# A quarter of the down weights multiplied in f32 straight from the raw buffer, and the gate/up biases added by VectorE

## The chip, the core and the metric

The kernel runs on one core of one Trainium2 chip. The metric is the device time of one execution in microseconds (us). Three executions of the kernel before gave a median of 1267.36 us (1266.95 to 1268.4).

The engines are named as in the profile: PE is TensorE, PEld its weight load, DVE VectorE, ACT ScalarE, POOL GpSimd and SP SyncE, which only issues DMAs here. A trailing q (SPq) is an engine's own queue.

## The reference

One encoder layer on 512 tokens of width 1024: a retention and pooling mixer, then a mixture of experts. Of the 32 experts each token takes the top 4. The work around the change is the expert block (cut):

```python
def moe(h, w_router, b_router, w_gu, b_gu, w_down, b_down):
    logits = (xt @ w_router + b_router)
    top_vals, top_idx = lax.top_k(logits, TOP_K)          # TOP_K = 4 of 32
    gates = jax.nn.softmax(top_vals, axis=-1)
    ...
    def expert_block(args):
        xblk, e = args
        gu = xblk @ w_gu[e] + b_gu[e]                     # 1024 -> 2048
        x_glu = jnp.minimum(gu[:, :F], SWIGLU_LIMIT)
        x_lin = jnp.clip(gu[:, F:], -SWIGLU_LIMIT, SWIGLU_LIMIT)
        act = x_glu * jax.nn.sigmoid(SWIGLU_ALPHA * x_glu) * (x_lin + 1.0)
        return act @ w_down[e] + b_down[e]                # 1024 -> 1024
```

All inputs are f32. The weights of an expert are 8 MB of `w_gu` and 4 MB of `w_down`, 384 MB for all 32.

## The kernel before, in words

**Front (0 to about 230 us).** The mixer, the router and the ranks of the tokens in their experts.

**Expert stages (about 240 to 1220 us).** The kernel goes through all 32 experts, 88 token places each. An expert's weights come as 12 chunks of 1 MB (128 x 2048 f32): chunks c = 0 to 7 are the gate/up rows, chunks 8 to 11 the down rows. The down chunks of an expert are loaded one stage late: stage s holds gate/up chunks 0 to 7 of expert s, then down chunks 8 to 11 of expert s-1. `nth(s, c)` numbers the chunks in that order; h is s // 2 and q is s % 2.

Every chunk takes the same way:
- SP waits until its raw slot is free and issues the load (`chunk`). There are 8 raw slots (SLOTS): six in the tile `ring`, two in `arena`. So chunk n can be issued once chunk n-8 has left its slot. SP issues strictly in order.
- ACT makes the f16 high part from the raw slot (`act_high`, L396).
- DVE makes the f16 low part from the raw slot and the high part (`dve_low`, L399). Then `low_ready` goes up, and with that the raw slot is free.
- PE multiplies the parts: three f16 products (high x high, low x high, high x low). For gate/up chunks these are 48 products of 88 columns (L420), for down chunks 12 products of 512 columns (L456). `chunk_used` goes up at the end. The high and low parts stand in six split slots.

Between the chunks of a stage stand, on PE: 16 bias products at its head (`pe_bias`, L441), two gathers of the next expert's tokens (L413, 32 products each; the first after chunk 4, in stage 1 after chunk 6; the second after chunk 7) and a small product for gates and rows (L427). On DVE: clamps of gate and up from PSUM (`dve_glu` L486, `dve_lin` L489), product L492, activation L495, its low part L501 and the one-hot tile of the gather (L461). On ACT: two copies of the gathered tokens (`columns`, L468), the sigmoid (L505), the high part of the activation (L498), two output copies (L508). All these orders are written out by hand: `stage` in each engine's block. In stage 1 ACT stands at `columns(2, 0, 1)` behind the high part of chunk 8, and waits there for PE's gather. POOL scatters an expert's 88 rows to `planes` in DRAM by an indirect DMA (L478).

**End.** When expert 30's rows are scattered, SP loads the planes (8 loads of 1 MB), DVE and PE add them up with the last expert's rows, and the final norm is written out.

Of the kernel before, what the change touches and what calls it, by code (L numbers as in the profile page):

```python
# [34 lines left out]
P = 128  # L35
# [14 lines left out]
def build_program(nc, x, norm_mix_w, w_in, ret_norm_w, w_pool, pool_scale, w_out, norm_ffn_w, w_router,  # L50
# [27 lines left out]
    with ExitStack() as ctx:  # L78
# [42 lines left out]
        bgu_raw = reg_p[0:64, 3168:5216]  # L121
# [32 lines left out]
        own_f = sm[:, 384 + RANKS:384 + RANKS + E]  # L154
        tri = sb("tri", [P, P], BF16)
        ones = sb("ones", [P, P], BF16)
        late = sb("late", [P, 2 * W])
        rw_sb = late[:, 0:W]
        wp_sb = late[:, W:2 * W].rearrange("p (h c) -> p h c", h=H)
        bgu_parts = late.bitcast(F16)  # L160
        own = sb("own", [P, E], F16)
        wr_sb = sb("wr_sb", [P, KD, E])
        br_sb = sb("br_sb", [P, E])
        ps_w = sb("ps_w", [P, H])
        eps_t = sb("eps_t", [P, 1])
# [37 lines left out]
        turned += [("qk", n) for n in range(2)] + [("qk", n) for n in range(2, 8)]  # L203
# [45 lines left out]
        bgu_high = sem("bgu_high")  # L249
        bgu_ready = sem("bgu_ready")  # L250
# [47 lines left out]
        low_ready = sem("low_ready")  # L298
        act32_ready = sem("act32_ready")
# [6 lines left out]
        glu_ready = sem("glu_ready")  # L306
        prod_ready = sem("prod_ready")
# [13 lines left out]
        more = {k: sem(f"more_{k}") for k in ("high", "low", "used", "onehot", "gathered", "xT",  # L321
# [61 lines left out]

        def load_gu(sp, k, e, slot):
            return sp.dma_start(raw(slot),
                                w_gu[0, bass.ds(e, 1), k * P:(k + 1) * P, :].rearrange("a p c -> (a p) c"))
# [51 lines left out]
        def pe_bias(pe, e):  # L438
            for b in range(GB):
                for j in range(PER):  # L440
                    pe.matmul(GU[:, b, j * CAP:(j + 1) * CAP], bgu_parts[:, gu_cols(b, j)],  # L441
                              own[:, bass.ds(e, 1)].to_broadcast([P, CAP]), start=(j == 0), stop=False,
                              skip_group_check=True)

        def pe_gu(pe, slot, q, k, b):
            for j in range(PER):
                mm = product(pe, GU[:, b, j * CAP:(j + 1) * CAP], split_of(slot), gu_cols(b, j), xT[:, q], k,
                             False, k == KD - 1)
# [34 lines left out]
        LIM = LIMIT / UNSCALE  # L483

        def dve_glu(dve):
            return dve.tensor_scalar(gub[:, :, 0], GU[:, :, 0:2 * CAP], LIM, UNSCALE, ALU.min, ALU.mult)  # L486

        def dve_lin(dve):
            return dve.tensor_scalar(gub[:, :, 1], GU[:, :, 2 * CAP:4 * CAP], LIM, -LIM, ALU.min, ALU.max)  # L489

        def dve_prod(dve):
            return dve.scalar_tensor_tensor(gub[:, :, 1], gub[:, :, 1], 1.0 / UNSCALE, gub[:, :, 0], ALU.add, ALU.mult)  # L492

        def dve_act32(dve):
            return dve.scalar_tensor_tensor(gub[:, :, 1], gub[:, :, 1], SCALE_A * UNSCALE, sig, ALU.mult, ALU.mult)  # L495
# [44 lines left out]
        def _(sp):  # L540
# [14 lines left out]
            for c in range(1, 5):  # L555
# [22 lines left out]
            def chunk(h, q, c):  # L578
# [5 lines left out]
                else:  # L584
                    sp.wait_ge(low_ready, nth(s, c) - SLOTS + 1)
# [17 lines left out]
            sp.wait_ge(mix_turned, H)  # L603
            for i in range(2):
                sp.dma_start(bgu_raw[32 * i:32 * i + E, :], b_gu[0]).then_inc(bgu_loaded, 16)
# [25 lines left out]
            def last_split():  # L631
                sp.wait_ge(low_ready, CH * E)
# [1210 lines left out]
```

## Time and profile before

| | |
|---|---|
| median of 3 runs | 1267.36 us |
| profiled execution, its own time | 1267.78 us |
| its span in the trace | 1266.0 us |
| PE busy | 1160.1 us (92%) |
| DVE busy | 1128.3 us (89%) |
| ACT busy | 924.4 us (73%) |
| POOL busy | 509.2 us (40%) |
| DMA | 458.07 MB, mean 362 GB/s |

The span is the traced part of one execution; 1.8 us lie around it. Busy shares are means over the whole span, and the stages have different limits. A duration in a row includes the start and end of the pipeline: DVE instructions of 2.3 us follow each other at 2.2 us. A DMA share of 1.00 means that all 16 DMA engines have a packet under way all the time.

### The profile page before, as it was taken

Reading aid. Unit: us, or ns where it says so; the run is one execution under the profiler, and the core shown is the slowest. Engines: PE = TensorE matmul, PEld = TensorE weight load, DVE = VectorE, ACT = ScalarE, POOL = GpSimd, SP = SyncE. Lnnn points to the kernel's source line nnn. Section 1 sums busy time; section 2 is a strip of 40 time slices with the busy share of each in tenths; the row PEclk is TensorE's granted clock in tenths of the full one; section 3 lists DMA queues with packets and bytes.
Section 4 is the critical chain, followed back from the end, with each engine's and each line's share of the span. In section 5 each row is a group of like instructions: output and inputs, shape, how many; then the busy total and the mean of one; then the engine's idle time right before and its main releaser. Section 6 shows DMA issues by size and latency. Waiting matters only on the chain.

```text
span 1266.0 us, 39786 instructions
## 1 busy us (share of the span) xinstructions
PE 1160.1 (92%) x17462; PEld 894.8 (71%) x17463; DVE 1128.3 (89%) x849; ACT 924.4 (73%) x819; POOL 509.2 (40%) x69
## 2 busy tenths in 40 slices
PE   5999999789999999999999999999999999999984
PEld 2455544777777777777777777777888777777741
DVE  5742454789999999999999999999999999999988
ACT  5332432579888888888888888888888888888852
POOL 0120300006666666666665551111166666622400
PEclk9999999799999999999999999999999999999998
DMA  9609331699999999999999999999999999999986
GB/s 350 218 20 353 126 134 58 229 371 378 420 416 416 418 413 417 418 418 417 416 417 414 419 418 418 414 418 413 415 416 419 417 411 420 418 412 409 418 324 255
DMA packets 73254, 458.07 MB, mean 362 GB/s; under 512 B 10076, under 2 KB 10588, under 8 KB 23632
## 3 DMA queue, kind: packets, MB, share of 16 engines
q1 hardware_dynamic: 68480, 445.30, 86.5%
q0 software_dynamic: 3472, 8.21, 1.7%
q8 instruction: 139, 2.28, 0.7%
q10 hardware_dynamic: 1152, 2.19, 0.5%
q14 instruction: 11, 0.09, 0.0%
HBM read 443.26 MB, written 24.77 MB: 370 GB/s over the span
## 4 chain that ended last, share of the span: by engine, by line
PE 44%; DVE 29%; issue 17%; DMA 6%; ACT 2%; DVEq 0%; SPq 0%; ACTq 0%; POOLq 0%
DVE ring L399 20%; PE ps L420 15%; PE ps L456 10%; PE ps L1093 8%; PE ps L1194 4%; PE ps L413 3%; DMA ring<-in_w_down_dram 2%; DMA arena<-in_w_down_dram 1%; DVE arena L492 1%; ACT ring L396 1%; DVE arena L486 1%; DVE arena L489 1%; DMA ring<-in_w_gu_dram 1%; DVE arena L501 1%; DVE arena L495 1%
## 5 line engine op out<-in xcount | busy, mean ns | idle before, releaser
L478 POOL DMA_INDIRECT planes<-arena,slot_row x31 | 484.2, 15619 | 586.8 <-ACT arena L508 586.8
L399 DVE SCALAR_TENSOR_TENSOR ring<-ring 128x2048 f16<-128x2048 f32 x290 | 657.5, 2315 | 15.0 <-ACT ring L396 14.7
L396 ACT ACTIVATE ring<-ring 128x2048 f16<-128x2048 f32 x290 | 543.1, 1905 | 46.4 <-DMA ring<-in_w_gu_dram 22.9
L420 PE MATMUL ps<-arena,ring 128*128 128x88 f16 x12288 | 505.1, 205 | 46.2 <-issue 27.8
L420 PEld LDWEIGHTS ps<-arena,ring 128*128 128x128 f16 x12288 | 489.2, 100 | 55.9 <-issue 43.2
L456 PE MATMUL ps<-ring,arena 128*88 128x512 f16 x1536 | 338.0, 379 | 5.6 <-DVE arena L501 2.6
L456 PEld LDWEIGHTS ps<-ring,arena 128*88 128x88 f16 x1536 | 181.4, 120 | 148.6 <-issue 6.0
L399 DVE SCALAR_TENSOR_TENSOR ring<-arena,ring 128x2048 f16<-128x2048 f32 x94 | 214.4, 2316 | 0.9 <-ACT ring L396 0.9
L396 ACT ACTIVATE ring<-arena 128x2048 f16<-128x2048 f32 x94 | 178.0, 1904 | 12.4 <-DMA arena<-in_w_down_dram 6.5
L413 PE MATMUL ps<-arena 128*128 128x88 f16 x2048 | 94.2, 207 | 10.9 <-issue 7.6
L413 PEld LDWEIGHTS ps<-arena 128*128 128x128 f16 x2048 | 86.6, 101 | 12.0 <-issue 11.9
L1093 PE MATMUL ps<-ring,arena 128*128 128x512 f16 x384 | 87.3, 386 | 0.9 <-DVEq L1416 0.9
L508 ACT ACTIVATE arena<-ps,slot_gate 88x512 f32<-88x512 f32 x62 | 38.9, 677 | 63.9 <-PE ps L456 46.5
L1093 PEld LDWEIGHTS ps<-ring,arena 128*128 128x128 f16 x384 | 38.0, 99 | 45.3 <-issue 2.7
L468 ACT ACTIVATE arena<-ps 128x704 f16<-128x704 f32 x64 | 47.7, 745 | 28.7 <-PE ps L413 28.5
L1194 PE MATMUL ps<-ring,arena 128*128 128x512 f32 x128 | 56.1, 594 | 0.0
L1194 PEld LDWEIGHTS ps<-ring,arena 128*128 128x128 f32 x128 | 23.9, 190 | 28.2 <-issue 28.2
L1395 DVE TENSOR_SCALAR var<-ss 128x1 f32<-128x1 f32 (+1 forms) x16 | 3.7, 232 | 37.7 <-ACT arena L840 30.6
L501 DVE TENSOR_TENSOR arena<-arena 128x704 f16<-128x704 f32 x32 | 29.3, 915 | 1.3 <-ACT arena L498 1.3
L441 PEld LDWEIGHTS ps<-own,late 128*128 128x128 f16 x512 | 24.6, 98 | 7.8 <-DVE arena L489 0.7
L498 ACT ACTIVATE arena<-arena 128x704 f16<-128x704 f32 x32 | 25.1, 784 | 6.4 <-DVE arena L495 6.4
L495 DVE SCALAR_TENSOR_TENSOR arena<-arena 128x704 f32<-128x704 f32 x32 | 29.3, 916 | 0.0
(153 smaller groups left out, 592.7 us busy)
## 6 DMA issues: line engine op xcount, KB each, us to landing
ring<-in_w_gu_dram SPq DMA_DIRECT2D x194, 1024.0 KB, 11.9
ring<-in_w_down_dram SPq DMA_DIRECT2D x96, 1024.0 KB, 12.1
arena<-in_w_gu_dram SPq DMA_DIRECT2D x62, 1024.0 KB, 12.5
arena<-in_w_down_dram SPq DMA_DIRECT2D x32, 1024.0 KB, 11.7
ring<-in_w_in_dram SPq DMA_DIRECT2D x4, 2048.0 KB, 12.4
ring<-planes SPq DMA_DIRECT2D x6, 1024.0 KB, 10.1
ring<-in_w_out_dram SPq DMA_DIRECT2D x2, 2048.0 KB, 8.5
arena<-in_x_dram SPq DMA_DIRECT2D x4, 512.0 KB, 11.6
```

The source lines that it names most:

```text
L396: return act.activation(split_of(slot)[:, 0, :], raw(r), ACT.Copy, scale=SCALE_W)
L399: return dve.scalar_tensor_tensor(split_of(slot)[:, 1, :], raw(r), SCALE_W, split_of(slot)[:, 0, :], ALU.mult, ALU.subtract)
L413: mm = pe.matmul(o, parts[:, i, t, d * P:(d + 1) * P], onehot[:, t, :], start=(t == 0), stop=(t == NT - 1), skip_group_check=True)
L420: mm = pe.matmul(o, w[:, i, cols], src[:, j, k, :], start=start and n == 0, stop=stop and n == 2, skip_group_check=True)
L456: mm = pe.matmul(ROWS[:, half, :], actT[:, j, f, :], w[:, i, col:col + 512], start=f == 0 and n == 0, stop=f == KD - 1 and n == 2, skip_gr ...
L468: return act.activation(xT[:, q, i].rearrange("p (a k) c -> p a (k c)", a=2), src, ACT.Copy)
L478: return pool.indirect_dma_start(out=planes, out_offset=bass.IndirectOffsetOnAxis(ap=rows, axis=0), in_=y_row[0:SCAT, :], in_offset=None, ...
L495: return dve.scalar_tensor_tensor(gub[:, :, 1], gub[:, :, 1], SCALE_A * UNSCALE, sig, ALU.mult, ALU.mult)
L501: return dve.tensor_tensor(actT[:, 1].rearrange("p (b j) c -> p b (j c)", b=GB), gub[:, :, 1], actT[:, 0].rearrange("p (b j) c -> p b (j c ...
L508: return act.activation(rows[0:CAP, half * 512:(half + 1) * 512], ROWS[:, half, :], ACT.Copy, scale=scale)
L1093: mm = pe.matmul(bank(("z", n)), lhsT, rhs, start=(k == 0 and step == 0), stop=(k == KD - 1 and step == 2))
L1194: mm = pe.matmul(bank(("out", m)), mixT[:, k, t * P:(t + 1) * P], wout(k)[:, half * 512:(half + 1) * 512], start=(k == 0), stop=(k == KD - 1))
```

## The change

Three things are changed:
- Chunk 8, the first of the four down chunks of a stage, is no longer split from stage 1 on. ACT and DVE pass over it (`unsplit`). PE takes it as f32 from its raw slot, with an f32 activation tile `nat` that ACT writes (`act_nat`, 128 x 176): four f32 products in place of twelve f16 ones. The last expert's down chunks, loaded behind stage 31, are all split as before. The raw slot of chunk 8 is free when PE has used it (`raw_free` waits for `chunk_used`), not when DVE has split it.
- The 16 bias products of a stage go. DVE adds the bias in a step of its own from PSUM to SBUF (`dve_bias`, 128 x 1408), and the two clamps then run in place in SBUF, one chunk later. PE may start the next stage when `dve_bias` is done. The biases are loaded at the start by ACT's queue, turned by four PE transposes behind the second turn of q and k, and copied by four DVE instructions into `bguT`.
- `ret_norm_w` and `w_pool` have tiles of their own, since the tile `late` of the bias parts is gone, and the steps that made those parts go too.

```diff
+        def unsplit(h, q, c):
+            return c == GU_CH and not (isinstance(h, int) and h == 0 and q == 0)
+        def raw_free(eng, h, q, c):
+            s = 2 * h + q
+            if c == GU_CH + SLOTS - CH and not (isinstance(s, int) and s == 1):
+                eng.wait_ge(chunk_used, nth(s, c) - SLOTS + 1)
+            elif c >= SLOTS:
+                eng.wait_ge(low_ready, splits(s, c - SLOTS))
+            else:
+                eng.wait_ge(low_ready, splits(s - 1, c + CH - SLOTS))
...
-        def pe_bias(pe, e):
...
+        def pe_down_native(pe, r, f):
+            for half in range(2):
+                col = (f % 2) * D + half * 512
+                mm = pe.matmul(ROWS[:, half, :], nat[:, f * CAP:(f + 1) * CAP], raw(r)[:, col:col + 512],
+                               start=f == 0, stop=False, skip_group_check=True)
+            return mm
...
+        def dve_bias(dve, e):
+            return dve.scalar_tensor_tensor(
+                gub.rearrange("p b h (j c) -> p b (h j) c", j=2), GU.rearrange("p b (j c) -> p b j c", j=PER), UNSCALE,
+                bguT[:, bass.ds(e, 1), :].rearrange("p a (b j) -> p (a b) j", b=GB).unsqueeze(3)
+                .to_broadcast([P, GB, PER, CAP]), ALU.mult, ALU.add)
 
         def dve_glu(dve):
-            return dve.tensor_scalar(gub[:, :, 0], GU[:, :, 0:2 * CAP], LIM, UNSCALE, ALU.min, ALU.mult)
+            return dve.tensor_scalar(gub[:, :, 0], gub[:, :, 0], LIMIT, None, ALU.min)
...
+        def act_nat(act):
+            return act.activation(nat[:, :], gub[:, 0, 1, :], ACT.Copy, scale=SCALE_W)
...
-                    sp.wait_ge(low_ready, nth(s, c) - SLOTS + 1)
+                    raw_free(sp, h, q, c)
...
+            act.dma_start(bgu_raw[:, :], b_gu[0].rearrange("e (q c) -> (e q) c", q=4)).then_inc(bgu_loaded, 16)
...
             def down(s, j, c):
-                pe.wait_ge(low_ready, nth(s, c) + 1)
+                if unsplit(s // 2, s % 2, c):
+                    r = raw_slot(s // 2, s % 2, c)
+                    pe.wait_ge(nat_ready, s)
+                    pe.wait_ge(slot_loaded[r], loaded(s // 2, s % 2, c))
+                    for f in range(2):
+                        mm = pe_down_native(pe, r, f)
+                    mm.then_inc(chunk_used, 1)
+                    return
+                pe.wait_ge(act_ready, s)
+                pe.wait_ge(low_ready, splits(s, c))
...
             def stage(s, q, last=False, more_meta=True):
+                pe.wait_ge(xT_ready, 2 * s + 2)
                 pe.wait_ge(gu_taken, s)
-                pe_bias(pe, s)
-                pe.wait_ge(xT_ready, 2 * s + 2)
...
                 else:
                     low(h, q, 10)
-                    taken(s, nth(s, GU_CH))
+                    biased(s, nth(s, GU_CH))
                     low(h, q, 11)
+                    clamped(s)
```

On PE, from the end of stage 1 to the first half of stage 2, before (L420 gate/up, L413 gather, L427 gates, L456 down, L441 bias):

```order
86 L420 MATMUL ps<-arena,ring 128x88 x48
87 L427 MATMUL ps<-meta,arena 88x3 x4
88 L413 MATMUL ps<-arena 128x88 x32
89 L456 MATMUL ps<-ring,arena 88x512 x48
90 L441 MATMUL ps<-own,late 128x88 x16
91 L420 MATMUL ps<-arena,ring 128x88 x240
92 L413 MATMUL ps<-arena 128x88 x32
```

and now (L436 gate/up, L429 gather, L443 gates, L472 the f32 products, L465 split down):

```order
85 L436 MATMUL ps<-arena,ring 128x88 x48
86 L443 MATMUL ps<-meta,arena 88x3 x4
87 L429 MATMUL ps<-arena 128x88 x32
88 L472 MATMUL ps<-ring,nat 88x512 x4
89 L465 MATMUL ps<-ring,arena 88x512 x36
90 L436 MATMUL ps<-arena,ring 128x88 x240
91 L429 MATMUL ps<-arena 128x88 x32
```

Twelve of the 48 down products became four f32 ones at the head of the down part, behind chunk 7 and the second gather, and the bias products are gone.

On SP, the loads of the loop's gate/up chunks 2 to 5 of an even stage with what they wait for, before:

```order
42 L385 ISA [waits low_ready]
43 L385 DMA ring<-in_w_gu_dram 128x2048
44 L585 REGISTER_ALU
45 L385 ISA [waits low_ready]
46 L385 DMA ring<-in_w_gu_dram 128x2048
47 L585 REGISTER_ALU
48 L385 ISA [waits low_ready]
49 L385 DMA ring<-in_w_gu_dram 128x2048
50 L585 REGISTER_ALU
51 L385 ISA [waits low_ready]
52 L385 DMA ring<-in_w_gu_dram 128x2048
```

and now:

```order
40 L401 ISA [waits low_ready]
41 L401 DMA ring<-in_w_gu_dram 128x2048
42 L398 REGISTER_ALU
43 L401 ISA [waits low_ready]
44 L401 DMA ring<-in_w_gu_dram 128x2048
45 L394 ISA
46 L401 ISA [waits chunk_used]
47 L401 DMA ring<-in_w_gu_dram 128x2048
48 L398 REGISTER_ALU
49 L401 ISA [waits low_ready]
50 L401 DMA ring<-in_w_gu_dram 128x2048
```

The load of chunk 4 takes the slot that chunk 8 of the stage before had; it now waits for PE, and the loads behind it wait with it.

## Rows read from the trace of the kernel before

**Rows 1.** Busy times by stretch: us, PE PEld DVE ACT POOL (instructions), PEclk, DMA share, GB/s
```profile
330.00:600.00 270.00, 253.88 (x4467) 210.02 (x4468) 270.00 (x159) 229.25 (x185) 185.41 (x9) 1.00 1.01 417
...
900.00:1200.00 300.00, 286.23 (x5015) 236.39 (x5015) 299.36 (x175) 257.75 (x202) 156.37 (x10) 1.00 1.01 416
```

**Rows 2.** What SP's queue waited for, 300 to 1200 us: total us, times, longest
```profile
SPq L385 <- DVE ring L399: 455.4, 232, 3.2
```

**Rows 3.** DMA issues of 300:400, 700:800, 1100:1200: count, KB, median us to landing
```profile
ring<-in_w_gu_dram SPq DMA_DIRECT2D x18, 1024.0 KB, 7.9
...
ring<-in_w_gu_dram SPq DMA_DIRECT2D x20, 1024.0 KB, 12.4
...
ring<-in_w_gu_dram SPq DMA_DIRECT2D x18, 1024.0 KB, 15.3
```

**Rows 4.** Groups by form, 300:1200: count, busy us, mean ns, idle before
```profile
L399 DVE SCALAR_TENSOR_TENSOR ring<-ring 128x2048 f16<-128x2048 f32 x262 | 594.2, 2317 | 0.8 <-ACT ring L396 0.5
...
L420 PE MATMUL ps<-arena,ring 128*128 128x88 f16 x11220 | 461.2, 205 | 39.9 <-issue 23.8 <-DVE ring L399 15.0
...
L456 PE MATMUL ps<-ring,arena 128*88 128x512 f16 x1392 | 305.9, 379 | 1.4 <-issue 1.4
...
L486 DVE TENSOR_SCALAR arena<-ps 128x704 f32<-128x704 f32 x29 | 26.6, 916 | 0.0
...
L441 PE MATMUL ps<-own,late 128*128 128x88 f16 x464 | 23.7, 202 | 0.0
```

**Rows 5.** The costliest groups of the page: the f32 products of the mixer
```profile
L1194 PE MATMUL ps<-ring,arena 128*128 128x512 f32 x128 | 56.1, 594 | 0.0
```

**Rows 6.** PE in time, stage 1: start us, us, instruction, count
```profile
281.20 1.41 PE L413 MATMUL ps<-arena 128*128 128x88 f16 x32
282.44 10.53 PE L456 MATMUL ps<-ring,arena 128*88 128x512 f16 x48
```

**Rows 7.** DVE in time, stage 1: chunk 8, then chunks 9 and 10
```profile
273.39 2.29 DVE L399 SCALAR_TENSOR_TENSOR ring<-ring 128x2048 f16<-128x2048 f32 x1
280.76 4.50 DVE L399 SCALAR_TENSOR_TENSOR ring<-ring 128x2048 f16<-128x2048 f32 x2 [5.08 <-ACT ring L396]
```

**Rows 8.** SP in time: loads of stage 2's chunks 4 and 5; landing of the second
```profile
275.88 0.33 SPq L385 DMA_DIRECT2D ring<-in_w_gu_dram  x1
...
283.65 0.34 SPq L385 DMA_DIRECT2D ring<-in_w_gu_dram  x1
...
ring<-in_w_gu_dram SPq DMA_DIRECT2D x1, 1024.0 KB, 4.8
```

**Rows 9.** Busy times of single microseconds, as rows 1
```profile
281.00:282.00 1.00, 1.00 (x31) 1.00 (x28) 1.00 (x1) 1.00 (x1) 0.00 (x0) 1.00 0.33 139
282.00:283.00 1.00, 1.00 (x19) 0.81 (x16) 1.00 (x2) 1.00 (x2) 0.00 (x0) 1.00 0.00 0
...
284.00:285.00 1.00, 1.00 (x6) 0.56 (x5) 1.00 (x1) 1.00 (x2) 0.00 (x0) 1.00 0.58 74
```

**Rows 10.** DVE in time, stage 2: chunks 6 and 7, then 8 and 9
```profile
305.01 4.50 DVE L399 SCALAR_TENSOR_TENSOR ring<-ring 128x2048 f16<-128x2048 f32 x2
309.42 4.50 DVE L399 SCALAR_TENSOR_TENSOR ring<-arena,ring 128x2048 f16<-128x2048 f32 x2
```

**Rows 11.** PE in time, stage 2: its down products
```profile
312.86 10.53 PE L456 MATMUL ps<-ring,arena 128*88 128x512 f16 x48
```

**Rows 12.** ACT, then PE in time, head of stage 1
```profile
260.13 0.75 ACT L468 ACTIVATE arena<-ps 128x704 f16<-128x704 f32 x1
...
261.08 4.55 PE L420 MATMUL ps<-arena,ring 128*128 128x88 f16 x112
```

**Rows 13.** The chain that ended last, pieces: start us, us, what
```profile
39.17 0.44 PE ps L1112 x4
...
1190.85 15.36 DMA ring<-in_w_down_dram
...
1212.07 2.21 DVE ring L399
1214.32 5.39 PE ps L456 x24
...
1221.84 5.09 DMA planes<-arena,slot_row
```

More of the change, by code:

```diff
@@ L202, in build_program @@
         turned = [("x", t, i) for t in range(NT) for i in range(2)]
-        turned += [("qk", n) for n in range(2)] + [("qk", n) for n in range(2, 8)]
+        turned += [("qk", n) for n in range(2)] + [("bgu", j) for j in range(4)] + [("qk", n) for n in range(2, 8)]
         turned += [("s", h, i) for h in range(H) for i in range(NT)]
@@ L319, in build_program @@
         scattered = sem("scattered")
-        more = {k: sem(f"more_{k}") for k in ("high", "low", "used", "onehot", "gathered", "xT",
+        more = {k: sem(f"more_{k}") for k in ("high", "low", "used", "onehot", "gathered", "xT", "biased",
                                               "glu", "lin", "prod", "sig", "act32", "ah", "act",
@@ L901, in _ @@
                 turned_h2(t)
-                if t == 1:
-                    act.wait_ge(bgu_loaded, 32)
-                    act.activation(bgu_parts[0:64, :], bgu_raw, ACT.Copy, scale=SCALE_W).then_inc(bgu_high, 1)
             first_high(5)
@@ L1066, in _, with turn_bgu @@
             pe.wait_ge(small_loaded, 16)
+            def turn_bgu():
+                pe.wait_ge(bgu_loaded, 16)
+                for j in range(4):
+                    take(pe, ("bgu", j))
+                    pe.transpose(bank(("bgu", j))[:, 0:P], bgu_raw[:, every_other(2 * P * (j // 2) + j % 2)], ident).then_inc(bgu_turned, 1)
             def turn_x(t):
@@ L1440, in _, with turned_bgu @@
             low_win(1, 0)
+            def turned_bgu():
+                for j in range(4):
+                    dve.wait_ge(bgu_turned, j + 1)
+                    dst = bguT[:, :, :].rearrange("p e (ql b qh r) -> p e qh ql b r", ql=2, b=2, qh=2)[
+                        :, :, :, :, j // 2, j % 2]
+                    ins = dve.tensor_copy(dst, bank(("bgu", j))[:, 0:P].rearrange(
+                        "p (e qh ql) -> p e qh ql", e=E, qh=2))
+                    free(ins, ("bgu", j))
             def rotate(n):
@@ L1625, in gates_and_meta, with biased @@
                 dve.sem_inc(routed, 1)
-            def taken(e, done, first=False):
+            def biased(e, done, first=False):
                 dve.wait_ge(chunk_used, done)
@@ L1685, in _ @@
             low(0, 1, 2)
-            taken(0, GU_CH, first=True)
+            biased(0, GU_CH, first=True)
             low(0, 1, 3)
+            clamped(0)
             low(0, 1, 4)
@@ L1698, in _ @@
             low(0, 1, 10)
-            taken(1, nth(1, GU_CH))
+            biased(1, nth(1, GU_CH))
             low(0, 1, 11)
+            clamped(1)
             stage(1, 0)
@@ L1722, in one @@
                 dve.wait_ge(more["used"], CH * (n - 1) + GU_CH)
+                dve_bias(dve, e).then_inc(more["biased"], 1)
+                dve.wait_ge(more["biased"], n)
                 dve_glu(dve).then_inc(more["glu"], 1)
```

94 lines of the change are left out of this document (44 added, 50 removed).

## The prediction

> **What bounds the kernel now.** I read the busy times by stretch first. From 330 to 1200 us DVE is busy all the time (270.00 of 270.00 us, 299.36 of 300.00), and so is the DMA: share 1.01 at 416 to 417 GB/s [rows 1]. PE stands at 286.23 of 300.00 us. Two resources at 100% can't both be the limit. The waits of SP's queue point at DVE: its loads waited 455.4 us for DVE's low parts [rows 2]. But that only says that every load goes out as soon as DVE frees a slot; it doesn't say that the load was urgent.
>
> What decides is the time from issue to landing: 7.9 us at 300 to 400, 12.4 at 700 to 800, 15.3 at 1100 to 1200 [rows 3]. The queue in front of the DMA engines grows for the whole run, so DVE frees slots faster than the DMA fills them. Sizes: a stage has 18 DVE instructions (12 low parts, one one-hot, five for the activation), and 900 to 1200 has 175, so DVE's stage is 18 / 175 x 300 = 30.86 us. The queue grew by 7.4 us in 800 us, 0.9%, so the DMA's stage is about 31.1 us. DVE began this part with landed chunks in front of it, and is eating them up; the DMA was the limit from the first full stretch on. The end agrees: the last long piece of the chain in front of the tail is a 15.36 us DMA of down weights from 1190.85 us [rows 13].
>
> So the time is: when the DMA becomes saturated for good (about 285 us), plus 31.1 us per stage of weights, which the change leaves at 12 MB, plus the tail from the last down chunks on. Work taken from ACT and DVE between these points is worth nothing by itself. What counts is whether loads are issued later or earlier.
>
> **The change part by part.**
>
> *DVE per stage.* A low part goes: the starts of rows 10 lie 4.41 us apart for two, so 2.20 us. `dve_bias` reads 1408 elements from PSUM. The 704-element clamp from PSUM has a mean of 916 ns, some 0.80 from start to start as with the low parts, and twice the elements give about 1.53 us [rows 4]. The clamps stay; in SBUF they cost between half and all of 0.80 us, since no row shows an f32 tensor-scalar between two SBUF tiles. Net: -2.20 + 1.53 - 2 x (0 to 0.40) = -0.7 to -1.5 us, so a stage of 29.4 to 30.2 us. It is now further below 31.1, and worth 0 to the end. ACT: minus a high part, plus 176 elements, also 0.
>
> *PE per stage.* PE's busy time is 286.23 / 300 x 30.86 = 29.4 us. Bias products: 23.7 / 29 = 0.82 us less. Twelve split down products: 305.9 / 1392 = 0.220 us each, 2.6 less. Four f32 products of 512 columns: the trace shows them as two instructions each of 56.1 / 128 = 0.438 us [rows 5], so 8 x 0.438 = 3.5 us more. Sum 29.5 us. PE's idle time of 1.4 us a stage, most of it "issue" [rows 4], on top is 30.9, still under 31.1: 0, but with little room.
>
> *The slot of chunk 8.* Before, DVE frees it; now PE does, behind chunk 7 and the second gather. Load n+8, chunk 4 of the next stage, waits for it, and chunks 5 to 7 stand behind it in SP's order though their slots are free.
>
> Stage 1, laid out. Before: the low part of chunk 8 runs at 273.39 [rows 7], its successor is issued at 275.88 [rows 8]. The next load (chunk 5) goes out at 283.65, since DVE had stood 5.08 us behind ACT, and the DMA engines ran dry: share 0.33 at 281 to 282, 0.00 at 282 to 283, and data again late in 284 to 285 (0.58, 74 GB/s) [rows 9]. So there is already a hole, from about 281.4 to 285.0. After: PE's start of stage 1 doesn't move, since it waits for the copy of the tokens that ACT ends at 260.88, and starts at 261.08 [rows 12]; the bias products stood beside that wait. So its down part starts at 282.44 as before [rows 6], the f32 products end at 285.9, and the load of chunk 4 goes out at 286.2 in place of 275.88. Its data begins 1.4 us later, 287.6 (from issue 283.65 to data at 285.0). The DMA runs dry one chunk earlier, at 281.4 - 2.6 = 278.8 (31.1 / 12 = 2.6 us a chunk). At 290 us the DMA was 5.0 us of service past chunk 4. Now it has 290 - 287.6 = 2.4 us past chunk 3, which is 0.2 before the end of chunk 4. It is 5.1 to 5.2 us behind, and nothing gives it back, since it is saturated from there: **+5.1 us**.
>
> Stage 2, by the same way. Low part 7 ends at 309.4; before, PE's down part starts at 312.86 [rows 10, 11], so the slot is free 3.45 + 3.5 = 7.0 us after low part 7, instead of 2.2. The DMA runs dry only if its queue at that time is shorter than 7.0 + 0.3 (issue) + 1.4 = 8.7 us. It was 7.9 to landing, of which 0.9 us is after the data (4.8 to landing less 1.4 and 2.5 of data): 7.0. After the first hole it is longer by 5.1, less 0.8 that DVE comes later in stage 1 (clamps in SBUF): 11.3. No hole. Where PE lags DVE by 3 us more, as it does in the middle, the need is 11.7, and 0 to 2 us are lost once or twice, until DVE and ACT have eaten up the landed chunks, which they do at 0.9 to 1.7 us a stage. I take **+1.0 us** (0 to 3). In the state where DVE and ACT wait for the DMA, 15 us are in the queue and the block of 7 to 10 us costs nothing.
>
> *Front.* Four f32 transposes on PE, whose chain runs unbroken there: like those of L1112, 0.44 us for four [rows 13]. The load of the biases, 0.25 MB, shares the DMA with the first x and w_in loads: at 400 GB/s 0.6 us at most, and 0 if it slips in; I take 0.5. DVE's four small copies and the removed steps at 190 to 212 us lie beside PE's products. **+0.9 us** (0.4 to 1.5).
>
> *Tail.* From the landing of stage 31's chunk 9 on, the chain goes over low parts, PE, output rows and the last scatter [rows 13]. In the last stage `dve_bias` stands ahead of low part 10 and the clamps ahead of low part 11, where both clamps stood ahead of low part 10: low part 10 is 0.1 earlier, low part 11 0.8 to 1.5 later. PE's last 24 products begin after 10 and need 11 only for the second half: 2.7 us of cover. 0 to 0.9 us there; the last expert's activation comes about 1 us later beside the loads of the planes. **+0.5 us**.
>
> Sum: 5.1 + 1.0 + 0.9 + 0.5 = 7.5 us on the profiled execution's 1267.78 us (span 1266.0 and 1.8 around it), 1275.3. That execution is 0.4 us over the median, so 1274.9 us.
>
> **The rivals.**
>
> *The DMA has room left (faster).* Then DVE's full use was the limit, as SP's waits say [rows 2], and the stage follows PE with its gaps or DVE: 30.2 to 30.6 us for 30.86. Over 29 stages that is 8 to 19 us, less the 7.5 above: 1255 to 1267, say 1260. For it: DVE has no idle time. Against it: the landing times double, and a DMA with room would have shrunk its queue. The Trainium skill (DMA: Bandwidth & Descriptors, Specifications) gives a fabric ceiling of 435 GB/s; by that rule, as an estimate, 416 would leave 4% and a stage could be 29.7 us. The trace has a share of 1.01 at 416, so it speaks against the rule's 4% here.
>
> *The first hole is partly made good (no change).* If PE reaches the f32 products earlier in stage 1, or if the DMA of before wasted as much between 285 and 330 us in small gaps, the loss shrinks to 0 to 2.5 us: 1267 to 1270.
>
> *PE becomes the limit, or holes at every stage (slower still).* PE's sum with its gaps is 30.9 us. If the f32 products wait for their weights, or gaps grow, a stage comes to 31.5 or more; and as PE lags, chunk 8's slot is freed later and SP's block outgrows the queue, so the DMA has a hole in every stage. It decides from a PE stage of 31.1 us. At 31.5 it is 29 x 0.4 = 12 us on top: 1287; at 32, 1300.
>
> **How the numbers follow.** Forecast 0.62 (1270 to 1281 by its own bounds: 5.1 less 2 to plus 1, 0 to 3, 0.4 to 1.5, 0 to 1.5, and 1 us for the layout); room in the DMA 0.12; made good 0.12; PE or repeated holes 0.14. What can be told from no change here is about 0.2%, 2.5 us. Faster: nearly all of the first rival and a little of the second, 0.13. Same: most of the second and the low edge of the forecast, 0.13. Slower 0.74. The range for 8 in 10 leaves out the far parts of both outer rivals: 1263 to 1287.
>
> **What would show it.** DMA share 1.0 and 416 GB/s from about 288 to 1220 us with no shorter stages: the DMA is the limit. An idle DMA of about 8.8 us between 278 and 288 us, with SP's chunk-4 load waiting for PE's f32 products: the first term. ACT and DVE with idle time that grows from nothing, both waiting for the DMA, from about the tenth stage: the saving had no taker. f32 products at 0.44 us an instruction; `dve_bias` near 1.5 us. I am wrong if stages come to less than 30.8 us (room in the DMA), or if the DMA share falls below 1.0 in the middle (PE's block).

## The result, and the profile after

The changed kernel takes 1273.59 us (median of 5 runs, 1272.86 to 1274.76), the kernel before, measured beside it, 1266.95 us (5 runs, 1266.69 to 1268.4). The ratio is 1.0052, with a 95% interval of 1.0039 to 1.0066: slower by some 6.6 us. The prediction said 1274.9 us. The two profiled executions, on which the accounts below rest, lie 5.8 us apart (spans of 1271.8 and 1266.0 us).

The busy times of the changed kernel by stretch, to be held against [rows 1] and [rows 9] (us, PE PEld DVE ACT POOL with instructions, PEclk, DMA share, GB/s):

```profile
280.00:281.00 1.00, 1.00 (x31) 1.00 (x28) 0.00 (x0) 1.00 (x1) 0.00 (x0) 1.00 0.42 172
281.00:282.00 1.00, 1.00 (x28) 1.00 (x25) 0.73 (x1) 1.00 (x2) 0.00 (x0) 1.00 0.00 0
285.00:286.00 1.00, 1.00 (x6) 0.40 (x5) 1.00 (x2) 1.00 (x1) 0.00 (x0) 1.00 0.00 0
286.00:287.00 1.00, 1.00 (x6) 0.58 (x5) 1.00 (x1) 1.00 (x2) 0.00 (x0) 1.00 0.41 66
318.00:322.00 4.00, 4.00 (x19) 2.10 (x18) 4.00 (x5) 2.64 (x4) 0.00 (x0) 1.00 0.55 179
349.00:353.00 4.00, 4.00 (x17) 1.82 (x16) 4.00 (x4) 3.72 (x3) 0.00 (x0) 1.00 0.77 269
330.00:600.00 270.00, 256.36 (x4354) 204.39 (x4351) 255.84 (x155) 213.54 (x179) 86.42 (x9) 1.00 1.01 414
900.00:1200.00 300.00, 284.86 (x4730) 224.59 (x4728) 285.56 (x175) 240.20 (x202) 94.89 (x11) 1.00 1.01 415
```

DVE has lost its full occupation (285.56 of 300 us, where it was 299.36) and the DMA has kept its own (share 1.01). The stage did not get shorter: from 600 to 1200 us DVE's one-hot steps, one in each stage, start 31.07 us apart on average, where they stood 30.94 apart before. What was saved on DVE had no taker. The first rows show where time was lost: the DMA engines stand still from about 280.4 to 286.6 us, again for some two microseconds in stage 2 (318 to 322) and for one in stage 3 (349 to 353).

Who kept the loads back, 300 to 1200 us (SP's queue: total us, times, longest), beside [rows 2]:

```profile
SPq L401 <- DVE ring L415: 234.8, 128, 3.8
SPq L406 <- DVE ring L415: 230.9, 110, 2.5
SPq L401 <- PE ps L472: 220.8, 29, 9.9
```

A new releaser stands there: 29 times, once a stage, SP's load of chunk 4 waits for PE's f32 products, on average 7.6 us. From issue to landing, 300:400, 700:800 and 1100:1200, beside [rows 3]:

```profile
ring<-in_w_gu_dram SPq DMA_DIRECT2D x18, 1024.0 KB, 12.6
...
ring<-in_w_gu_dram SPq DMA_DIRECT2D x18, 1024.0 KB, 15.2
...
ring<-in_w_gu_dram SPq DMA_DIRECT2D x18, 1024.0 KB, 15.0
```

Before, this time grew through the run (7.9, 12.4, 15.3). Now it is 12.6 us at 300 to 400 and stands at 15 in the two later stretches: the queue in front of the DMA no longer grows, and ACT waits for data, 160 us in all from 300 to 1200. Groups by form, 300 to 1200 us, beside [rows 4] (count, busy us, mean ns, idle before):

```profile
L415 DVE SCALAR_TENSOR_TENSOR ring<-ring 128x2048 f16<-128x2048 f32 x249 | 564.2, 2285 | 29.5 <-ACT ring L412 27.9 <-issue 1.5
...
L472 PE MATMUL ps<-arena,nat 128*88 128x512 f32 x120 | 54.7, 598 | 0.8 <-issue 0.8
...
L500 DVE SCALAR_TENSOR_TENSOR arena<-ps,bguT 128x1408 f32<-128x1408 f32 x29 | 46.9, 1618 | 0.0
...
L506 DVE TENSOR_SCALAR arena<-arena 128x704 f32<-128x704 f32 x29 | 15.1, 520 | 0.0
...
L521 ACT ACTIVATE nat<-arena 128x176 f32<-128x176 f32 x28 | 9.6, 341 | 0.0
```

The new operations cost what was expected: `dve_bias` 1.62 us (1.54 to the next start), a clamp in SBUF 0.52 (0.43 to the next start) where it read 0.916 from PSUM, one of the two instructions of an f32 product 54.7 / 120 = 0.456 us. The Trainium skill (VectorE: DVE Perf Modes, "The perf-mode tier table" and, under it, "Why PSUM operands drop a tier") gives f32 `tensor_scalar` in SBUF twice the plain rate, and f32 from PSUM the plain rate only; this case's trace agrees, 520 against 916 ns.

PE in time in stages 1 and 2, beside [rows 6] and [rows 12] (start us, us, instruction, count, idle before):

```profile
261.63 5.66 PE L436 MATMUL ps<-arena,ring 128*128 128x88 f16 x140 [1.81 <-ACT arena L484]
...
281.86 3.64 PE L472 MATMUL ps<-ring,nat 128*88 128x512 f32 x8
285.33 6.85 PE L465 MATMUL ps<-ring,arena 128*88 128x512 f16 x31
...
315.01 3.64 PE L472 MATMUL ps<-arena,nat 128*88 128x512 f32 x8
318.49 7.93 PE L465 MATMUL ps<-ring,arena 128*88 128x512 f16 x36
```

SP in time, beside [rows 8], stage 1 and stage 2:

```profile
285.67 0.98 SPq L401 DMA_DIRECT2D ring<-in_w_gu_dram  x2
...
318.82 0.92 SPq L401 DMA_DIRECT2D arena<-in_w_gu_dram  x2
```

Each follows the end of the f32 products by 0.2 us. The chain that ended last, front and tail, beside [rows 13]:

```profile
45.49 0.45 PE ps L1140 x4
45.97 0.61 ACT ring L834
46.62 0.39 PE ps L1094
...
1167.84 15.00 DMA ring<-in_w_down_dram
...
1213.83 3.47 PE ps L472 x8
1217.30 7.78 PE ps L465 x36
```

In front, turning the biases puts an ACT copy and a product, 1.1 us with the gaps around them, into a chain that ran unbroken. At the end, PE's last down part but one starts with the f32 products.

Last, the chain of 900 to 1200 us by line, before and then now:

```profile
by line: DVE ring L399 39.3%; issue 32.3%; DMA ring<-in_w_down_dram 10.3%; DMA arena<-in_w_down_dram 5.1%; DVE arena L492 2.8%; DVE arena L486 2.6%; DVE arena L489 2.5%; DVE arena L501 2.0%; DVE arena L495 1.8%; ACT ring L396 1.3%; DVE aren
...
by line: PE ps L436 23.1%; DMA ring<-in_w_down_dram 19.4%; issue 17.8%; PE ps L465 10.4%; DVE ring L415 8.5%; DMA arena<-in_w_down_dram 4.9%; PE ps L472 4.7%; PE ps L429 3.9%; DVE arena L500 3.2%; ACT ring L412 3.2%; DVE arena L512 1.8%; DV
```

Before, most of it is DVE, with DMA pieces in between; now PE and the DMA take turns. So neither kernel is paced by the DMA alone, and this must be kept in mind in all that follows.

To see where the difference comes up, I counted the 8 KB packets of the weights in each trace from the last backwards, 128 to a load of 1 MB, and took the time at which each load's worth had been moved, less the same time in the kernel before. This is the lag, in us; the time that heads a column is that of the kernel before. The experiments told below stand in the same table:

```
kernel               261   279   288   313   318   349   411   690  1001  1215
changed              1.5   2.3   4.4   1.8   5.1   6.5   7.7   7.4   8.5   6.4
bias_only            1.4   1.5   0.0   0.5   1.0   2.4   3.7   9.7  15.1  18.4
native_only         -0.3   0.7   4.1   1.7   2.6   3.3   3.7   4.7  16.8  21.0
native_nobias       -1.3  -0.4   4.5   1.9   3.5   4.5   5.3   5.6   6.1   3.9
late_native          0.9   3.4   0.1   0.8   1.1   2.2   6.9   6.9   7.4   6.2
before_cols         -0.2  -0.2  -4.3  -3.7  -3.7  -3.4  -3.7  -3.8  -3.4  -4.6
after_swap           1.3   2.6   2.6   1.3   2.3   2.8   3.2   2.6   3.7   2.1
```

The changed kernel has its 7.7 us at 411 us and then runs at the old pace. The right-hand columns are to be read roughly, since the 16 DMA engines don't work on the same load at the same time: by the landings that the semaphores tell, the changed kernel lags by 7.5 us at 411, 6.0 at 690, 5.3 at 1001 and 5.6 at its last load, and `native_only` by 11.4 at 1001.

### The profile page after: what moved, and what is told of

It reads as the page before. It is cut to its first block, busy times and chain, and to the rows that moved or that the text cites. A ratio compares the mean times of both kernels' runs of the same rounds, so it can differ in the third digit from the quotient of the medians.

```text
span 1271.8 us, 38614 instructions
## 1 busy us (share of the span) xinstructions
PE 1169.9 (92%) x16830; PEld 869.6 (68%) x16831; DVE 1088.2 (86%) x851; ACT 877.2 (69%) x818; POOL 370.8 (29%) x69
## 4 chain that ended last, share of the span: by engine, by line
PE 44%; DMA 20%; DVE 16%; issue 15%; ACT 4%; DVEq 0%; SPq 0%; ACTq 0%
PE ps L436 15%; DMA ring<-in_w_down_dram 15%; PE ps L1121 8%; PE ps L465 8%; DVE ring L415 7%; DMA arena<-in_w_down_dram 4%; PE ps L1223 4%; ACT ring L412 3%; PE ps L472 3%; PE ps L429 3%; DVE arena L500 3%; DVE arena L512 1%; DMA arena<-in_x_dram 1%; DVE arena L506 1%; PE ps L1159 1%
## 5 line engine op out<-in xcount | busy, mean ns | idle before, releaser
L415 DVE SCALAR_TENSOR_TENSOR ring<-ring 128x2048 f16<-128x2048 f32 x274 | 620.6, 2285 | 44.3 <-ACT ring L412 42.7
L412 ACT ACTIVATE ring<-ring 128x2048 f16<-128x2048 f32 x274 | 519.1, 1907 | 114.9 <-DMA ring<-in_w_down_dram 71.0
L494 POOL DMA_INDIRECT planes<-arena,slot_row x31 | 345.8, 11154 | 728.7 <-ACT arena L531 728.7
L436 PE MATMUL ps<-arena,ring 128*128 128x88 f16 x12288 | 508.0, 205 | 46.2 <-issue 23.0
L436 PEld LDWEIGHTS ps<-arena,ring 128*128 128x128 f16 x12288 | 491.2, 100 | 64.7 <-issue 38.4
L465 PE MATMUL ps<-ring,arena 128*88 128x512 f16 x1164 | 258.1, 381 | 2.6 <-DVE arena L524 2.6
L465 PEld LDWEIGHTS ps<-ring,arena 128*88 128x88 f16 x1164 | 140.2, 121 | 127.3 <-issue 22.6
L415 DVE SCALAR_TENSOR_TENSOR ring<-arena,ring 128x2048 f16<-128x2048 f32 x79 | 179.5, 2286 | 12.7 <-ACT ring L412 12.5
L412 ACT ACTIVATE ring<-arena 128x2048 f16<-128x2048 f32 x79 | 150.6, 1906 | 56.8 <-DMA arena<-in_w_down_dram 41.4
L429 PE MATMUL ps<-arena 128*128 128x88 f16 x2048 | 93.1, 206 | 10.8 <-issue 7.5
L429 PEld LDWEIGHTS ps<-arena 128*128 128x128 f16 x2048 | 85.7, 101 | 11.8 <-issue 11.8
L472 PE MATMUL ps<-ring,nat 128*88 128x512 f32 x128 | 58.2, 597 | 0.0
L472 PE MATMUL ps<-arena,nat 128*88 128x512 f32 x120 | 54.7, 598 | 0.8 <-issue 0.8
L500 DVE SCALAR_TENSOR_TENSOR arena<-ps,bguT 128x1408 f32<-128x1408 f32 x32 | 51.8, 1618 | 0.0
L472 PEld LDWEIGHTS ps<-ring,nat 128*88 128x88 f32 x128 | 18.9, 157 | 26.1 <-issue 26.1
L1425 DVE TENSOR_SCALAR var<-ss 128x1 f32<-128x1 f32 (+1 forms) x16 | 3.7, 231 | 38.4 <-ACT arena L861 30.6
```

What stands on the lines that cost most here:

```text
L412: return act.activation(split_of(slot)[:, 0, :], raw(r), ACT.Copy, scale=SCALE_W)
L415: return dve.scalar_tensor_tensor(split_of(slot)[:, 1, :], raw(r), SCALE_W, split_of(slot)[:, 0, :], ALU.mult, ALU.subtract)
L429: mm = pe.matmul(o, parts[:, i, t, d * P:(d + 1) * P], onehot[:, t, :], start=(t == 0), stop=(t == NT - 1), skip_group_check=True)
L436: mm = pe.matmul(o, w[:, i, cols], src[:, j, k, :], start=start and n == 0, stop=stop and n == 2, skip_group_check=True)
L472: mm = pe.matmul(ROWS[:, half, :], nat[:, f * CAP:(f + 1) * CAP], raw(r)[:, col:col + 512], start=f == 0, stop=False, skip_group_check=True)
L494: return pool.indirect_dma_start(out=planes, out_offset=bass.IndirectOffsetOnAxis(ap=rows, axis=0), in_=y_row[0:SCAT, :], in_offset=None, ...
```

## The experiments

Theory: the DMA is the limit, the change moves work between engines that have just enough room, and pays for holes in the load stream while the queue is short. Rivals: DVE or PE limits, and the loss comes from their stage.

**The two halves.** `bias_only` is the changed kernel with chunk 8 split again in every stage, `native_only` the kernel before with chunk 8 in f32 and its bias products kept on PE.

```diff
 def unsplit(h, q, c):                      # bias_only
-    return c == GU_CH and not (isinstance(h, int) and h == 0 and q == 0)
+    return False
...
```

```diff
+                if unsplit(s // 2, s % 2, c):  # native_only, on the kernel before
...
+                        mm = pe_down_native(pe, r, f)
...
                 pe_bias(pe, s)
```

> The changed kernel with chunk 8 split again in every stage; only the bias step on DVE is left of the change. Theory (two limits close to each other, DMA 31.1 us a stage and DVE 30.86): DVE's stage rises by 1.54 for the bias step and falls by 2 x 0.36 for the clamps in SBUF, to 31.7 us, which is above the DMA, so DVE becomes the limit: 29 x (31.7 - 30.86) = 24 us more, plus 1.8 in the front: 1292 us (1287 to 1297), landing times falling instead of growing. Rival (DMA alone sets the stage and DVE's time doesn't matter): about 1269.

Measured 1290.14 us, ratio 1.0178 (1.0164 to 1.0192), as expected. Its busy times:

```profile
600.00:900.00 300.00, 275.96 (x4653) 222.70 (x4652) 300.00 (x182) 245.46 (x209) 201.99 (x11) 1.00 1.01 408
```

DVE is full, its stage 31.67 us (its one-hot steps start at 617.42 and 649.09), above the DMA's 31.1; landing times stay at 8.5, 8.0, 8.1 us. The DMA's busy share still reads 1.01, but at 408 GB/s: the share alone doesn't tell that the DMA is the limit. What tells DVE from the DMA here is the lower rate together with a time to landing that stays at 8 us.

> The kernel before with the f32 product of chunk 8 alone; the biases stay products on PE. Theory (the slot of chunk 8, freed by PE, blocks SP's queue): the changed kernel lost 1.8 us in the front to the biases' load and transposes and about 5 us of DMA service in stages 1 to 4; this one keeps only the second, so 1266.95 + 5 = 1272 us (1270.5 to 1273.5), with the DMA idle near 281 to 286 and again at about 317 and 350 us. Rival (the late bias step on DVE and the later clamps made the loss): then this kernel is within 1.5 us of the kernel before. Rival (the DMA has room): faster, below 1264, since DVE's stage falls by 2.2 us.

Measured 1293.91 us, ratio 1.0216 (1.0194 to 1.0239): the expectation was wrong by 22 us. To 500 us the lag was 3.7 us, a little under the 5 expected; then it grew to 21. The chain of 900 to 1200 us by line, and the busy times:

```profile
by line: PE ps L439 48.2%; PE ps L475 23.3%; PE ps L482 10.4%; PE ps L432 8.2%; issue 7.4%; PE ps L460 2.0%; PE ps L446 0.5%
```

```profile
900.00:1200.00 300.00, 277.78 (x4791) 223.44 (x4788) 269.77 (x157) 229.60 (x194) 9.11 (x9) 1.00 0.98 401
```

The whole chain is PE: gate and up (L439), down (L475, L482), gathers (L432) and its own gaps. A stage was 31.97 us from 600 to 1200 us. By the prediction's rows PE needed 29.5 + 0.82 + 1.4 = 31.7 here, so I had set a limit aside that I could have worked out.

**Is it the bias products, then?** The same kernel without them, so that its output lacks the gate and up biases:

```diff
 def pe_bias(pe, e):
+    return
...
-                             False, k == KD - 1)
+                             k == 0 and j == 0, k == KD - 1)
```

> Before with chunk 8 read in f32 by PE, the biases neither added nor multiplied: PE's bias products are left out and nothing stands in their place, so the output lacks the gate and up biases. The variant with the bias products in place took 1293.91 us, its stages 31.98 us in the middle, limited by PE. Theory (PE's queue was the limit there, and the bias products were 0.82 us of each stage on it): a stage is back at the DMA's 31.1 us, and the time is that of the changed kernel less its front cost of 1.8 us, 1271 to 1274 us. Rival (the f32 products read from the raw buffers slow DVE, ACT or the weight loads by themselves, whatever stands in PE's queue): it stays at 1285 us or more.

Measured 1271.87 us, ratio 1.003 (1.002 to 1.0041), at the lower end of the theory. The chain of 900 to 1200 us, and the busy times:

```profile
by line: DMA ring<-in_w_down_dram 34.6%; DVE ring L418 21.8%; DMA arena<-in_w_down_dram 21.4%; issue 14.6%; ACT ring L415 6.5%; DVE arena L514 2.7%; DVE arena L511 2.6%; DVE arena L508 1.7%; ACT arena L490 1.6%; DVEq L1590 0.3%; SPq L409 0.
```

```profile
600.00:900.00 300.00, 283.02 (x4877) 227.26 (x4875) 278.57 (x166) 239.22 (x202) 116.39 (x10) 1.00 1.01 416
```

The chain runs over DMA again, at 416 GB/s. The f32 products are harmless until 0.82 us of other PE work stands beside them; over 29 stages that makes 22 us. This is shown: one edit, 22 us, and the limit moved from PE to the DMA.

**When the f32 chunk starts.** `late_native` is the changed kernel with chunk 8 split up to stage 3 and in f32 from stage 4 on.

```diff
 def unsplit(h, q, c):
-    return c == GU_CH and not (isinstance(h, int) and h == 0 and q == 0)
+    return c == GU_CH and not (isinstance(h, int) and h < 2)
...
```

> The changed kernel, but chunk 8 is split as before in stages 1 to 3 and taken as f32 from stage 4 on. Theory (SP's block costs DMA service only while DVE is behind the DMA and the queue is short): in stages 1 to 3 DVE's stage is 31.7 us and its lag grows a little, so the queue is shorter at stage 4 than in the kernel before and the block costs there what it cost in stages 1 to 3: the loss is put off, 1272 to 1274 us, DMA holes at stages 4 to 6. Rival (the loss belongs to stage 1, where ACT stood behind PE's gather): the loss is gone but for the front, 1268.5 to 1270.

Measured 1272.73 us, ratio 1.0041 (1.0027 to 1.0055), as expected. The lag is 2.2 us at 349 us and 6.9 at 411: the loss isn't tied to stage 1 but comes in the first stages in which SP is blocked by PE, wherever they are. Its hole at 378 to 384:

```profile
378.00:384.00 6.00, 6.00 (x22) 2.73 (x21) 6.00 (x6) 3.80 (x7) 1.35 (x1) 1.00 0.76 261
```

**Taking the holes away.** `after_swap` lets SP issue chunk 5 ahead of chunk 4 from stage 2 on, so that one load goes out while chunk 4's slot is still held by PE. `before_cols` is the kernel before with ACT's `columns(2, 0, 1)` behind the high parts of chunks 9 and 10 of stage 1, which removes the hole of [rows 9]; `after_swap_cols` has both on the changed kernel.

```diff
-                    for c in range(CH):                                    # after_swap
+                    for c in (0, 1, 2, 3, 5, 4, 6, 7, 8, 9, 10, 11):
                         chunk(h, q, c)
```

```diff
             high(0, 1, 8)                                                  # before_cols
-            columns(2, 0, 1)
             high(0, 1, 9)
             high(0, 1, 10)
+            columns(2, 0, 1)
```

> The kernel before, but in stage 1 ACT makes the high parts of chunks 9 and 10 before it copies the gathered tokens of expert 2, so it no longer stands 7 us behind PE's gather. Theory (the time is the moment from which the DMA is saturated, plus 31.1 us a stage): the DMA hole of 281.4 to 285.0 us goes, because loads 5 and 6 of stage 2 go out about 4 to 5 us earlier: 3 to 4 us faster, 1263.5 us. Rival (DVE sets the stage): DVE's idle 5.1 us before chunk 9 goes as well, and it gains 5 us at once: 1262 us. Rival (neither, PE is in the way): same as before within 1 us.

Measured 1263.8 us, ratio 0.9969 (0.9959 to 0.998), as expected. The microsecond that had a DMA share of 0.00 [rows 9] now reads:

```profile
282.00:283.00 1.00, 1.00 (x12) 0.62 (x9) 1.00 (x2) 1.00 (x3) 0.00 (x0) 1.00 1.04 418
```

The 4.3 us gained by 288 us are still there at the end (3.4 to 4.6), and it is the version that beats both kernels. It doesn't tell what limits the kernel before: the same edit takes away DVE's 5.08 us behind ACT [rows 7], and the rival by which DVE sets the stage had expected 1262 us against the theory's 1263.5, too close to part them.

> The changed kernel, but from stage 2 on SP issues the load of chunk 5 ahead of chunk 4, the one that waits for PE's f32 products. Theory (the loss is SP's order: loads whose slots are free stand behind the one that isn't): the DMA has one more chunk in its queue when the block comes, 2 us less hole in stage 1, 1.8 in stage 2, 0.9 to 1.5 in stages 3 and 4: 4 to 5 us faster than the changed kernel, 1269 us (1267.5 to 1270.5). Rival (the loss is that chunk 8's slot itself comes free late, in whatever order): no change, 1273.6. Rival (chunk 4 landing after chunk 5 makes ACT and DVE wait once a stage, which they can't make good): slower than 1275.

> The changed kernel with both: chunk 5 issued ahead of chunk 4, and in stage 1 ACT's copy of the gathered tokens behind the high parts of chunks 9 and 10. Theory: the low part of chunk 9 is done about 5 us earlier in stage 1, so the load of chunk 5 goes out before the DMA runs dry and the hole there shrinks by about 2.6 us more: 1266 us (1264.5 to 1268). It stays above the kernel before with that ACT order alone (1263.8) by the front's 1.8 us and what is left of the block.

`after_swap` measured 1271.94 us, ratio 1.0041 (1.0028 to 1.0054), and `after_swap_cols` 1271.19, 1.0032 (1.002 to 1.0044). The direction is as expected and the size is not: 1.7 and 2.4 us less than the changed kernel's 1273.59, where some 4.6 and 7.6 were expected. The holes did shrink: the lag stays near 3 us instead of 7.5. But the lag no longer carries over to the end as it stands: the last load of `after_swap` lands 2.3 us late, and its span is 3.7 us longer than before (1269.7). In the changed kernel the two agree, 5.6 and 5.8 us. So the smaller holes are worth 3.3 us at the last landing and 2.1 of span. The chain of its 900 to 1200 us mixes PE and DMA:

```profile
by line: PE ps L436 25.2%; issue 14.2%; PE ps L465 10.4%; PE ps L472 8.2%; DMA arena<-in_w_gu_dram 7.8%; DVE ring L415 6.4%; PE ps L429 5.2%; DMA ring<-in_w_down_dram 4.9%; DMA arena<-in_w_down_dram 4.7%; DMA ring<-in_w_gu_dram 3.6%; ACT ri
```

With the DMA ahead by 4 us, PE is the next limit at once. That the remaining 1.4 us are PE's backlog at the end agrees with this chain, but no run took it apart.

**Relieving the DMA.** In `before_less` and `after_less` half the columns of down chunks 9 and 11 are not loaded, so a stage has 11 MB in place of 12.

```diff
 def load_dn(sp, j, e, slot):
...
+            if j % 2:
+                return sp.dma_start(raw(slot)[:, 0:D], src[:, 0:D])
             return sp.dma_start(raw(slot), src)
```

> The kernel before, with half of the columns of down chunks 9 and 11 not loaded (their raw slots keep old data there): 11 MB a stage in place of 12, so a DMA stage of 28.5 us. Theory (DVE at 30.86 us is almost as slow as the DMA at 31.1, and was busy without a break to about 1200 us): next to nothing is gained, 1265.5 us (1263.5 to 1267), and the landing times fall to below 7 us. Rival (the DMA alone sets the time): 29 x 2.6 us = 75 us less, or down to whatever comes next.

Measured 1264.45 us, ratio 0.9979 (0.997 to 0.9988): DVE full (300.00 of 300), landing at 8 us, and only 3 us gained by 8% less to load. DVE's one-hot steps stand 30.85 us apart to the end. In the kernel before they do so too, 30.85 or 30.86 us apart from 300 up to some 880 us, and from 300 us to the end DVE's low parts wait 1.9 us in all. So DVE sets the pace of the stage there, and the DMA with its 31.1 us falls behind by a quarter of a microsecond in each. The 3 us are all that the DMA alone holds back in the kernel before.

> The changed kernel with the same 11 MB a stage. Theory (what the change took from DVE and PE is real, and the DMA took it): now it shows. DVE's stage is 29.5 us (11 low parts at 2.20, bias 1.54, two clamps at 0.43, three steps at 0.80, one-hot 0.43), PE's 29.3 and its gaps of about 1 us: 30.3 to 30.5 us a stage against 31.1, 29 x 0.7 = 20 us less than the changed kernel, 1253 us (1248 to 1258), faster than the kernel before with the same relief by about 12 us. Rival (SP's block behind chunk 8 keeps the DMA and all from going faster): 1268 or more.

Measured 1271.95 us, ratio 1.0044 (1.0031 to 1.0057): wrong by 19 us. The chain of 900 to 1200 us, and the busy times:

```profile
by line: PE ps L438 42.1%; PE ps L467 20.7%; DVE ring L417 10.0%; PE ps L474 9.3%; issue 8.2%; PE ps L431 6.9%; DVE arena L502 1.1%; DVE arena L517 0.5%; PE ps L445 0.4%; DVE arena L508 0.3%; DVE arena L511 0.3%; DVE arena L526 0.3%; DVE ar
```

```profile
600.00:900.00 300.00, 283.83 (x4823) 227.02 (x4822) 287.70 (x174) 238.97 (x202) 16.85 (x10) 1.00 0.95 382
```

The number is the one that the rival named, by which SP's block behind chunk 8 holds everything back (1268 or more). The trace speaks against it: with DMA (0.95) and DVE (287.70) both idle at times, PE carries the chain, and it never waits for DVE. Its idle time is its own (PE's waits, 600 to 1200 us):

```profile
PE ps L438 <- issue: 24.6, 25, 1.9
```

A stage is 31.05 us from 600 to 1200 us (DVE's one-hot steps again), about 29.5 of them PE's busy time and 1.6 its gaps: the same as the DMA's 31.1.

**Relieving PE as well.** Of `after_less`'s 36 split down products a stage, 12 are left out.

```diff
                 for n, (i, j) in enumerate(((0, 0), (0, 1), (1, 0))):
+                    if f >= 2 and n == 1:
+                        continue
                     mm = pe.matmul(ROWS[:, half, :], ...
```

> The changed kernel with half the columns of down chunks 9 and 11 not loaded (11 MB a stage, as in the run that took 1271.95 us), and with 12 of the 36 split down products left out (the low tokens with the high weights for f from 2 on), about 12 x 0.22 = 2.6 us of PE's stage. Theory (three limits lie side by side: with the DMA at 11 MB PE with its gaps set 31.1 to 31.4 us a stage): PE's stage falls to 28.6 and DVE's 29.4 to 30.2 us is the limit; 29 stages x 1.1 to 1.8 us less than 1271.95 give 1220 to 1240 us, DVE busy all the time in the middle. Rival (something shared, such as the order of slots and waits between SP, ACT, DVE and PE, held the stage at 31 us, not PE's own work): 1265 to 1272 us.

Measured 1225.57 us, ratio 0.9679 (0.9661 to 0.9697), as the theory said: 46 us less than `after_less`. The edit also frees chunk 8's slot earlier, so it doesn't part PE's work from SP's block by itself; with the chain and the waits of `after_less` it does.

```profile
600.00:900.00 300.00, 276.82 (x4973) 225.63 (x4971) 299.89 (x184) 251.47 (x213) 194.59 (x11) 1.00 0.99 402
```

DVE is full again, and its one-hot steps start 29.5 us apart. So the change does take 1.4 us a stage from DVE. It was worth nothing because the DMA and PE each stand at 31.1.

## Why the prediction was right, and where its steps were not

The time, the sign and the reason in the main (no room in the DMA, so DVE's saving has no taker; PE's hold on chunk 8's slot opens holes) were right. That the sum came so close is in part luck, since several terms erred and cancelled. Step by step:

- **The limit.** Right that the DMA had no room: share 1.01 at 414 to 415 GB/s to 1200 us, ACT and DVE with idle time, no shorter stage. Too strong was "the DMA was the limit from the first full stretch on": in the kernel before DVE set the pace of the stages (`before_less`), and in the changed one PE stands beside the DMA (`after_less`). Not right either was that the DMA was saturated for good from about 285 us: in the kernel before, 290 to 313 us had 374 GB/s at a share of 0.98; the changed one ran at 421 there. 23 us x 47 / 421 = 2.6 us were made good. That is the second rival, in part, and the prediction's "nothing gives it back" was wrong by it: the lag falls from 4.4 to 1.8, in `native_only` from 4.1 to 1.7.
- **DVE.** 1.53 predicted for `dve_bias`, 1.54 measured; clamps at the lower end of their bounds, 0.43. A stage predicted at 29.4 to 30.2 us, 29.5 in `after_less_pe`. Right, and worth 0.
- **The first hole, +5.1.** The mechanism was right almost to the microsecond: load issued at 285.67 (286.2 predicted), DMA dry from 280.4 (278.8) to 286.6 (287.6). But it added only 2.9 us to the 1.5 already there, 4.4 where the prediction's front and hole make 6.0. About 1 us is the earlier issue and data. The rest is a fault of logic: PE's start in stage 1 hardly followed the front's delay (261.63 for 261.08, 0.55 us), so the hole ends when it ends, and earlier lag of the loads disappears in it. `native_only`, with no lag in front of the hole, stands at 4.1 behind it.
- **The front, +0.9.** Undersized (1.8 us at 170 to 230 us: 0.7 is there by 45 us, and an ACT copy and a product that come into PE's chain add 1.1) and yet worth almost nothing: in `bias_only` a lag of 1.5 is 0.0 behind stage 1's hole. Two errors that cancelled; they should not have been added in a row.
- **Stage 2 has no hole, later ones +1.0 (0 to 3).** This step failed. Stage 2's hole took 3.3 us (1.8 to 5.1), though some of it came back by 339 us (4.4); stage 3's took 2.1 (to 6.5), and the lag was 7.7 at 411. I had the DMA's queue at 11.3 us there; what was made good before (2.6) and the smaller first hole (2.2 less) left about 6.5, against a block that I had put at 8.7. The block itself was longer too: PE's down part began at 315.01, not 312.86, because DVE came 1.4 us later with low part 7, for which PE waited, and PE then stood 0.7 us in a gap of its own. `native_only`, whose f32 products begin at 312.01 in stage 2, lost 0.9 us there.
- **Holes altogether.** The term "holes" was 6.1 and front 0.9; the lag at 690 us is 7.4. `late_native` gets 6.9 with the holes elsewhere, which speaks for more than luck: load time is lost until the queue is longer than PE's block, and no more after that. By this reading the need (my 11.7) was right and its distribution over stages was not. `after_swap`, whose block is one load shorter, settles at 3, which agrees; that the bound is this one was argued and not tested by itself.
- **The tail, +0.5.** The last load lands 5.6 us late and the span is 5.8 longer: +0.2 for +0.5.
- **PE, 30.9 under 31.1, with little room.** Too low by some 0.15 (31.05 in `after_less`), which hardly showed in the sum, since it came out equal to the DMA's. It did show in two of my expectations: `native_only` and `after_less` were wrong by 22 and 19 us because I treated PE as out of play. The first rival did so too: it took a stage of 30.2 to 30.6 us, though the prediction's own sum had PE at 30.9. And the rival "PE becomes the limit" was 0.82 us of bias products away.

So two of the terms were mis-sized in opposite directions (the first hole 2.2 us too large, the later holes some 5 too small), the front's was void, 2.6 us were made good, and the total stood. Each half of the change alone costs 2%: the f32 products overload PE, the bias step overloads DVE, and each makes room for what the other brings.

## What to carry to other kernels

When the DMA's share is 1.0, read the time from issue to landing over the run. Where it grew (7.9 to 15.3 us here), the DMA was slower than the engine that set the pace and about to take over; where it stood at 15, with ACT waiting for data, the DMA had taken over; where it stood at 7 to 13 (`bias_only`, `before_less`, `after_less`, `native_only`), an engine set the pace. Before taking work off the fullest engine, write down the stage time of every engine with its own gaps, since a saving is worth only the distance to the next limit: here nothing, as the DMA's 31.1 us lay above DVE's 30.86 already. And a delay that comes ahead of a hole isn't added to it: whatever ends the hole sets the time.

## What the runs showed that I had not expected

- Three limits within 1%: DMA 31.1 us, DVE 30.86 us and PE 31.1 us with its gaps (29.5 busy). Relieving the DMA alone gave 0.2% (`before_less`), relieving all three 3.2% (`after_less_pe`).
- PE's "issue" gaps were real: 24.6 us in 25 gaps in 600 us of `after_less` ahead of gate and up, up to 1.9 us each. In `before_less`, where PE also waits for DVE, the same row has 4.8 us. No engine releases PE from them, but the DMA's rows show what they go with. One gap of `after_less` (PE in time, then the DMA queues of 337.5 to 340 us):

```profile
337.50 0.99 PE L438 MATMUL ps<-arena,ring 128*128 128x88 f16 x21
340.21 0.96 PE L438 MATMUL ps<-arena,ring 128*128 128x88 f16 x20 [1.73 <-issue]
...
q8 instruction: 1, 0.02, 2.4%
```

  This packet of 16 KB on the queue that carries instructions ran from 337.93 to 338.89 us. All 45 gaps of over 0.3 us in 300 to 1200 us of `after_less` end 1.0 to 1.7 us after such a packet, and so do the 39 of the kernel before, the 29 of the changed one and all 370 of the twelve traces, where chance would give about 33. So PE in all likelihood stands there until the next piece of its program has come. Why the piece comes late, and in some stages only, no run shows.
- At a DMA share of 1.01 the rate was 407 to 408 GB/s in `bias_only` and 416 in the kernel before; at 0.98 it was 374 from 290 to 313 us. The share is no measure of the room that is left. The Trainium skill (DMA: Bandwidth & Descriptors, Specifications) puts a limit of about 358 GB/s on what one core gets from HBM; its section "Bandwidth" has that as each core's share when both cores of a pair stream. This case's trace is above it, with 416 held over 870 us on one busy core.
